# Attention steps placed between the quarters of the input projection's column blocks, and one ring for both kinds of weight halves

## The reference, cut to what matters

```python
def token_mixers(h, w_in_l, ...):                      # per layer
    gate_b, gate_c, u, q, k, v, g_conv, g_attn = jnp.split(h @ w_in_l, IN_SPLITS, axis=-1)
    y_conv = (gate_b * short_conv(gate_c * u, conv_w_l, conv_b_l)) @ w_conv_out_l
    ...                                                 # q, k rotated for the sample only
    o = rms_norm(diff_attention(q, k_all, v_all, lam), subln_g_l) * (1 - lam_init)
    y_attn = o.transpose(0, 2, 1, 3).reshape(b, n, ATTN_W) @ w_attn_out_l
    merged = jax.nn.sigmoid(g_conv) * y_conv + jax.nn.sigmoid(g_attn) * y_attn
    return merged @ w_out_l, k, v
```

## Time and profile before

| | |
|---|---|
| median of 3 runs | 1264.48 us (1263.8 to 1265.05) |
| the profiled execution | 1265.79 us, span 1264.0 us |
| PE busy | 1131.8 us, 90% of the span |
| DVE busy, ACT busy | 855.1 us (68%), 712.9 us (56%) |
| DMA | 332.56 MB, mean 263 GB/s |
| chain that ended last | PE 80%, DVE 7%, DMA 5%, ACT 4%, issue 3% |

### The profile page before, as it was taken

One profiled execution on the slowest core, in us unless ns is written; L12 is line 12 of the kernel. 1 busy time (PEld: TensorE's weight loads), 2 busy tenths in 40 slices (PEclk: granted clock), 3 DMA queues, 4 the chain that ended last, 5 costly groups with the idle time before them and its releaser, 6 DMA issues.

```text
span 1264.0 us, 15771 instructions
## 1 busy us (share of the span) xinstructions
PE 1131.8 (90%) x5573; PEld 910.0 (72%) x5573; DVE 855.1 (68%) x1227; ACT 712.9 (56%) x1018; POOL 149.4 (12%) x140
## 2 busy tenths in 40 slices
PE   4699999889799999799999989449999999999980
PEld 1588885468689889588886478438888788788870
DVE  1575686645675455585676845539889889889964
ACT  1444455534544444444445644538888888888862
POOL 5040002000360000340002000340000000000001
PEclk9799999999899999899999979769999999999995
DMA  9776657985259746565746964069999999999952
GB/s 327 285 262 231 200 168 270 386 325 185 92 164 410 274 160 204 148 203 197 233 166 216 387 212 152 0 227 337 375 381 384 373 381 383 373 388 378 375 211 100
DMA packets 165848, 332.56 MB, mean 263 GB/s; under 512 B 6528, under 2 KB 27120, under 8 KB 165792
## 3 DMA queue, kind: packets, MB, share of 16 engines
q1 hardware_dynamic: 158288, 307.78, 69.2%
q0 software_dynamic: 7472, 24.03, 5.6%
q10 hardware_dynamic: 32, 0.01, 0.0%
HBM read 314.48 MB, written 17.30 MB: 262 GB/s over the span
## 4 chain that ended last, share of the span: by engine, by line
PE 80%; DVE 7%; DMA 5%; ACT 4%; issue 3%; POOL 0%; SPq 0%; ACTq 0%; DVEq 0%; POOLq 0%
PE bank L1269 24%; PE bank L1271 23%; PE bank L1270 23%; DMA raw<-in_ada_w 4%; PE bank L1458 2%; ACT w_hi L534 2%; PE bank L1353 1%; DVE xT_lo L850 1%; PE bank L1413 1%; DVE x L863 1%; DVE w_lo L815 1%; ACT xT_hi L557 1%; PE bank L1561 1%; PE bank L1402 1%; PE bank L1582 1%
## 5 line engine op out<-in xcount | busy, mean ns | idle before, releaser
L815 DVE TENSOR_TENSOR w_lo<-raw,w_hi 128x1024 fp32r<-128x1024 f32 (+1 forms) x484 | 567.6, 1204 | 226.5 <-ACT w_hi L534 224.6
L534 ACT ACTIVATE w_hi<-raw 128x1024 fp32r<-128x1024 f32 (+1 forms) x504 | 500.2, 1008 | 359.4 <-PE bank L1271 359.1
L1269 PE MATMUL bank<-w_hi,xT_hi 128*128 128x512 f32 (+1 forms) x1056 | 409.4, 388 | 25.9 <-DVE w_lo L815 12.4
L1271 PE MATMUL bank<-w_lo,xT_hi 128*128 128x512 f32 (+1 forms) x1056 | 404.1, 383 | 0.0
L1270 PE MATMUL bank<-w_hi,xT_lo 128*128 128x512 f32 (+1 forms) x1056 | 403.9, 382 | 0.0
L1269 PEld LDWEIGHTS bank<-w_hi,xT_hi 128*128 128x128 f32 x1056 | 200.4, 190 | 67.4 <-issue 14.6
L1271 PEld LDWEIGHTS bank<-w_lo,xT_hi 128*128 128x128 f32 x1056 | 200.2, 190 | 35.1
L1270 PEld LDWEIGHTS bank<-w_hi,xT_lo 128*128 128x128 f32 x1056 | 200.7, 190 | 33.3
L1269 PE MATMUL bank<-w_hi,hT_hi 128*128 128x512 f32 x360 | 142.6, 396 | 3.4 <-issue 3.4
L1271 PE MATMUL bank<-w_lo,hT_hi 128*128 128x512 f32 x360 | 141.3, 392 | 0.0
L1270 PE MATMUL bank<-w_hi,hT_lo 128*128 128x512 f32 x360 | 141.0, 392 | 0.0
(11 more groups left out here) (233 smaller groups left out, 860.2 us busy)
## 6 DMA issues: line engine op xcount, KB each, us to landing
raw<-in_w_in SPq DMA_DIRECT2D x52, 1024.0 KB, 5.1
raw<-in_ada_w SPq DMA_DIRECT2D x48, 1024.0 KB, 11.4
raw<-in_moe_w_gate SPq DMA_DIRECT2D x32, 1024.0 KB, 7.4
raw<-in_moe_w_up SPq DMA_DIRECT2D x32, 1024.0 KB, 8.1
raw<-in_moe_w_down SPq DMA_DIRECT2D x32, 1024.0 KB, 7.9
raw<-in_moe_w_gate SPq DMA_DIRECT2D x16, 768.0 KB, 8.9
raw<-in_moe_w_up SPq DMA_DIRECT2D x16, 768.0 KB, 7.6
raw<-in_moe_w_down SPq DMA_DIRECT2D x16, 768.0 KB, 7.8
```

The lines of the kernel that those rows point to most:

```text
L534: nc.scalar.activation(w_hi[:, unit, 0:n], raw[:, r, at:at + n], ACT.Copy).then_inc(hi_done, 1)
L815: V.tensor_tensor(w_lo[:, unit, 0:n], raw[:, ring(q, s)[0], at:at + n], w_hi[:, unit, 0:n].bitcast(F32), ALU.subtract).then_inc(lo_done, 1)
L1269: pe.matmul(o, hi, wh, start=start, stop=False)
L1271: return pe.matmul(o, hi, wl, start=False, stop=stop)
```

## The change

The attention stage is gone. Each of the 13 blocks of `w_in` is taken in its four quarters, so that a layer has 52 quarters, numbered 0 to 51 (`tick` in the code; quarter `4*pos + unit`). From quarter 8 on every even quarter holds a step of the attention's pipeline, 20 steps in quarters 8 to 46; one step's work on PE is in two pieces, ahead of the quarter's matmuls (`step_begun`: score matmul 0 and p times V) and behind them (`step`: the transposes of q and k, score matmul 1, the transposes of p). The order of `w_in`'s blocks is now q, k, v, q, k, v, three convolution blocks, four gate blocks. The scores of both halves lie in one bank, p and the output in one bank, and so each job waits for the copies of the job before it. The ring is given out by halves in the order of use: in quarters 5 to 35 of layer 0 three of four hold a conditioning half, in layer 1 every odd one. The convolution's four chunks follow quarters 37, 39, 41 and 43. ACT's Sigmoid for the first gate block (`LATE_GATE`, block 9) comes behind the last exponential, in quarter 40. The amounts of arithmetic and of bytes stay.

```diff
+        qkT = sb("qkT", [P, 2, 3 * T])
...
-        def s_bank(j, i):
-
-            return bank[j % 2 + 6 * i]
+        QK, ADA, SCORES, PO = 2, 3, 4, 5
+
+        def scores(i):
+
+            return bank[SCORES][:, 2 * T * i:2 * T * (i + 1)]
...
+        STEP0, STEPS = 2 * PARTS, JOBS + 4
+        CONV0 = 9 * PARTS + 1
+        LATE_GATE = 9
+
+        def step_at(tick):
+            t = (tick - STEP0) // 2
+            return t if tick % 2 == 0 and 0 <= t < STEPS else None
...
+        def half_at(l, tick):
+            if not PARTS < tick < 9 * PARTS:
+                return None
+            if l == 0:
+                return None if tick % PARTS == 0 else 2 * QUAD * quads(l)[0] + tick // PARTS * 3 - 3 + tick % PARTS - 1
+            return None if tick % 2 == 0 else 2 * QUAD * quads(l)[0] + (tick - PARTS) // 2
...
+            needed = [(PARTS * (r - 1) + 2 * half, 0, ("weights", turn0[l] * SLOTS + r, half))
+                      for r in range(Q_LAYER * SLOTS) for half in range(2)]
+            for tick in range(PARTS * IN_BLOCKS):
+                n = half_at(l, tick)
+                if n is not None:
+                    needed.append((tick, 1, ("ada", n // 2, n % 2)))
+            stream += [entry for _, _, entry in sorted(needed)]
...
                 # ACT
+                for tick in range(PARTS * IN_BLOCKS):
+                    pos, unit = divmod(tick, PARTS)
+                    if unit == 0 and pos and pos - 1 != LATE_GATE:
+                        evacuated(pos - 1)
+                    hi(*slot(l, pos + 1), (unit,))
...
+                    if step_at(tick) is not None:
+                        step(step_at(tick))
+                    if tick == STEP0 + 2 * JOBS:
+                        evacuated(LATE_GATE)
+                    if quad_done(l, tick) is not None:
+                        ada_copy(quad_done(l, tick))
+                    if conv_at(tick - 1) is not None:
+                        conv_part(conv_at(tick - 1))
...
                 # DVE
+                    if step_at(tick) is not None:
+                        step_begun(step_at(tick))
+                    lo(*slot(l, pos + 1), (unit,))
+                    if step_at(tick) is not None:
+                        step(step_at(tick))
...
+                    if tick == CONV0 - 1:
...
+                        then(V.tensor_tensor(work[:, B_GC, :], work[:, B_GC, :], work[:, B_U, :], ALU.mult))
+                        dve.sem_inc(gcu_ok, 1)
+                    if conv_at(tick) is not None:
+                        conv(conv_at(tick))
+                    if conv_at(tick - 1) is not None:
+                        conv_rests(conv_at(tick - 1))
...
                 # PE
+                def step_begun(t):
+                    j = t - 1
+                    if 0 <= j < JOBS:
+                        pe.wait_ge(j_qkT, JOBS * l + j + 1)
+                        if j >= 1:
+                            pe.wait_ge(j_exp, JOBS * l + j)
+                        scored(j, 0).then_inc(j_s0, 1)
...
+                        if j >= 1:
+                            pe.wait_ge(j_oc, JOBS * l + j)
+                        for k in range(keys(j) // T):
+                            ins = pe.transpose(bank[PO][:, k * T:(k + 1) * T], p_buf[:, y, k * T:(k + 1) * T], ident[:, :])
+                        ins.then_inc(j_pT, 1)
...
+                    for unit in range(PARTS):
+                        tick = PARTS * pos + unit
+                        if step_at(tick) is not None:
+                            step_begun(step_at(tick))
+                        columns(*slot(l, pos), (unit,), outs, COL)
+                        if quad_turned(l, tick) is not None:
+                            i = quad_turned(l, tick)
+                            pe.wait_ge(j_pTc, JOBS * l + min((tick - STEP0) // 2 - 2, JOBS))
+                            ada_turn(i, bank[PO][:, 3 * T:3 * T + 4 * G * QUAD])
+                        if step_at(tick) is not None:
+                            step(step_at(tick))
+                        if half_at(l, tick) is not None:
+                            ada_half(half_at(l, tick))
+                        if conv_at(tick) is not None:
+                            conv_transposes(conv_at(tick))
```

More of the change, by code:

```diff
@@ new lines, in quad_done, with quad_turned, quads_kept @@
+        def quad_done(l, tick):
+            h = half_at(l, tick)
+            return None if h is None or h % (2 * QUAD) < 2 * QUAD - 1 else h // (2 * QUAD)
+        def quad_turned(l, tick):
+            if tick % 2 == 0:
+                return None
+            return quad_done(l, tick - 1) if quad_done(l, tick - 1) is not None else quad_done(l, tick - 2)
+        def quads_kept(l, tick):
+            return quads(l)[0] + sum(quad_turned(l, i) is not None for i in range(tick))
+        stream = [("ada", n // 2, n % 2) for n in range(2 * QUAD)]
@@ L278, in _, with free @@
         def _(sp):
[L279 to L282 removed]
+            def free(i):
+                if i >= 2 * SLOTS:
+                    kind, n, half = stream[i - 2 * SLOTS]
                     if kind == "ada":
[L284 removed]
+                        sp.wait_ge(ada_sum, 2 * n + half + 1)
                     else:
                         sp.wait_ge(lo_done, PARTS * n + 2 * half + 2)
[L288 to L294 removed]
@@ new lines, in source @@
+            def source(kind, n, half):
+                if kind == "ada":
+                    return columns(a["ada_w"][n // ADA_BLOCKS], half, n % ADA_BLOCKS * COL, COL)
+                l = int(n >= turn0[1] * SLOTS)
+                r = n - turn0[l] * SLOTS
+                if r < IN_BLOCKS:
+                    return columns(a["w_in"][l], half, ORDER_IN[r] * COL, COL)
+                if r < Q_LAYER * SLOTS:
+                    name, k0 = (("w_conv_out", 0), ("w_attn_out", 0), ("w_attn_out", 4), ("w_out", 0), ("w_out", 4))[r - IN_BLOCKS]
+                    return rows(a[name][l], half, k0, k0 + 4)
+                e, j = divmod(r - Q_LAYER * SLOTS, PER_EXPERT)
+                return expert_part(j, half, a["ffn_w_gate"][0][:, e * FF:(e + 1) * FF], a["ffn_w_up"][0][:, e * FF:(e + 1) * FF],
+                                   a["ffn_w_down"][0][e * FF:(e + 1) * FF, :])
@@ new lines, in _, with of, first_rows @@
+            for i, (kind, n, half) in enumerate(stream):
+                free(i)
+                r, part, _ = seat(i)
+                fill(r, part, *source(kind, n, half))
+            q = turn0[1] + Q_LAYER
+            def of(e):
+                return tuple(a[n][0, bass.ds(e, 1)].rearrange("e d f -> (e d) f")
+                        for n in ("moe_w_gate", "moe_w_up", "moe_w_down"))
+            def first_rows():
+                sp.wait_ge(x_sent, 16 * 2 * G)
+                x_load(0)
+                sp.wait_ge(gx_t, 1)
+                x_load(1)
```

590 lines of the change are left out of this document (253 added, 337 removed).

## The result

The changed kernel takes 1287.67 us (median of 4 runs, 1286.19 to 1291.82) beside 1264.14 us for the kernel before on the same chip: ratio 1.0185, 95% interval 1.0171 to 1.0199, 23.5 us slower. The prediction of 1272 us had the sign right and the size wrong; the time lies above its range (1255 to 1282). The profiled execution took 1288.15 us, span 1286.4 us, with PE busy for 1154.9 us (90%), DVE 856.0 (67%) and ACT 712.4 (55%).

A forecast was written before the change was run, and what follows sets the result against it. PE was taken as the bound, except in the attention stages, where it idles (layer 0's limited by DMA). Prize -27.5, (a) and (b) +15.6, waits +17.3, clock +1.9 gave +7.3 on 1264.5: 1272 us, range 1255 to 1282.

The forecast's parts named there:

- The prize: Both layers' attention stages: PE's idle time, a wait before the broadcast and slow matmuls afterwards go away, 27.5 us gained.
- (a): A job's two score matmuls no longer side by side on PE: 0.29 us more per job, 4.6 us per layer.
- (b): Each return of PE from float32 work to weight matmuls: 0.08 us, 40 returns, 3.2 us per layer.
- The waits: PE waiting on ACT and DVE, mostly in quarters 37 to 44 and at turns: 8.3 and 9.0, together 17.3 us.
- layer 1's two turns: PE's turns of `ada_turn` behind quarters 21 and 37 wait for DVE's copy of p's transposes, 1.0 us each.
- (c): PE's clock drops to the lower level after a wait of 4 us: 1.9 us, at even odds in each layer.
- The ring by halves: Weight ring and its DMAs, costed at nothing; PE waits 1 to 3 us if six halves don't bridge block 1.
- Rival 3: Each score matmul alone costs as much as the pair, in every even quarter: 10.6 us more, 1282.6 us; chance 0.13.
- Rival 1: Faster: ACT and DVE keep up in quarters 36 to 44, some 1.5 us waited per layer, 1255.6 us; chance 0.24.
- Rival 2: No change: waits of 5 us per layer and no clock loss, or lower (a), 1264.5 us; chance 0.15.
- Rival 4: Layer 0's weight ring runs dry on DMA in blocks 1 to 4, 6 us or more, 1278 us; chance 0.06.
- Exponentials and p come just in time: Up to quarter 35, while odd quarters hold a conditioning half, ACT's and DVE's answers reach PE without a wait.

The follow-up runs named there:

- The best version: `e13_dve_reordered` with the rotations of blocks 0 and 1 moved back to the odd quarter: 1250.1 us, ratio 0.9882 to the kernel before.
- e13_dve_reordered: Changed kernel with score pair ahead, later Sigmoids, early Sqrt table, and DVE's chunks, conditioning addition and rotations reordered: 1257.2 us, ratio 0.9933 to the kernel before.
- e3_one_score: The changed kernel without score matmul 1, both softmaxes reading matmul 0's scores: 1285.3 us, ratio 1.0160 to the kernel before.
- e9_step_first_one_score: The changed kernel with DVE's step ahead of `lo` and score matmul 1 left out: 1260.7 us, ratio 0.9977 to the kernel before.

## Why the prediction was wrong, step by step

**The prize, 27.5 us: right.** The best version has two layers 14.5 us shorter than before. It pays for its returns (about 0.16 x 80 = 12.8 us) and still waits some 2 us, so that the idle time won is about 29 us.

**(a), the two scores apart: the term that was mis-sized most, 9.2 us.** Each of the two takes alone what the pair takes (0.415 and 0.63 us), so that 0.52 us a job was due for the matmul alone where the sum had 0.29, gaps included. The balance below leaves 17 us for it. The experiments stand on both sides of that: a score left out gave 0.67 us a job, the pair kept together 0.43, 14 us. My reason for the low end, that the whole-array matmuls show no exposed weight load, does not bear on the question: each half of the pair was never cheap, the two ran at the same time. The prediction had cited a page of the Trainium skill for just this (TensorE: Matmul & The Clock Gate, "Why this matters for your kernels": slices of fewer than 128 rows run concurrently, one alone takes as long as a full-height one) and weighed it below a doubtful reading of rows; the trace agrees with the page as to the two running at once, 0.626 us for one and 0.63 for two.

**(b), 0.08 per return, 6.4 us in all: too low by half.** I read only the first interval behind a transpose. The whole return is 0.11 to 0.17, and 0.09 come ahead where a half or a score follows the weight matmuls: 0.16 to 0.17 a quarter, about 13 us.

**The waits, 17.3 us: right, mechanism and size.** Quarter 42 was put at 4.1 and took 3.9; 44 at 1.35 and took 1.35; 40 at 1.0 and took 0.6; layer 1's two turns at 1.0 and waited 0.7 each. PE's waits inside the two layers sum to 15.3 us.

**(c), 1.9 us at even odds: it came in both layers,** 2.2 us in each of the quarters 43 alone.

**Not in the sum:** the table load ahead of the norms (2.2 us). I had followed the load that the change adds ahead of the Sigmoids, not the one that is due when Sqrt comes back. The ring by halves was costed at nothing, and no run shows more: the stretch ahead of layer 0's `w_in`, 1.4 us shorter in the changed kernel, takes 43.8 to 45.3 us in the kernels with the new ring and 44.4, 45.5 and 46.7 in the three with the old.

With (a) as what is left over, the measured sum is -27.5 + 17 + 13 + 15.3 + 4.5 + 2.2 - 2.0 = +22.5 us, and 22.4 were measured between the spans. The prediction had +7.3: (a) and (b) are 14 us of the 15 that it missed, (c) and the table 5 more, the waits and the 2.0 won at the ends 4 less.

**The rivals.** Rival 3 (scores as dear as the pair), at 0.13, had the mechanism of (a), and its sign, single scores of 0.4 and 0.6 us, is what the trace shows; by the sum it alone gave 1282.6, and (b), (c) and the table lie beyond it. Rival 1 fell: ACT and DVE do not keep up in quarters 36 to 44. Rival 2 had neither the waits' full size nor the clock loss that came. Rival 4 did not come in the changed kernel, where no `w_in` quarter waits for `raw`; its kind of wait came once, in `e13_dve_reordered`, not by the DMA rate but because slots were freed late.

**What failed in the form of the sum.** The terms were added as if each stood alone. `e3_one_score` shows that they don't: with one score left out altogether the time was still 1285, so with (a) merely as cheap as I had it, it would have been no less, and not the 1280 that the sum gives. The turns and the exponentials would have been waited for, and the clock would have fallen behind the waits. "Exponentials and p come just in time" stood in the prediction; read on, it says that PE has no slack there to win. So the right price of (a) closes the balance, but (a) by itself did not put the time above the range: the price of the split and the way round through `lo` bind together, and only the edit of both (`e9_step_first_one_score`) gave the time back.

## What to carry to other kernels

Here a pair of matmuls on different rows of the array was one unit of time (0.63 us for two, 0.63 for one): before splitting such a pair over two places, price each half as the whole pair. When a dependent chain is spread between the parts of a dense stream, draw the way round through every queue that it crosses and put each answer ahead of the instruction that waits for the stream (`hi`, `lo`), not behind it; only then does PE's saving show. The idea of the change was sound (1.2% faster in the end): its order and the split pair were what cost 3% against that.

## What the runs showed of the hardware that I had not expected

DVE and POOL hinder each other: a rotation's `tensor_tensor` with two operands in SBUF took 2.6 us beside POOL's and 0.41 without it. The Trainium skill (GPSIMD Engine Reference, "Specifications") says that POOL's SBUF interfaces are shared with VectorE, with contention for instructions with two SBUF inputs; here the trace agrees, and the price is a wait for nearly the whole of POOL's instruction.

Leaving the weight matmuls for float32 work and coming back has a price on both sides. The return costs 0.11 to 0.17 us, much the same behind one transpose, p times V, a score or a conditioning half; another 0.09 comes ahead when the work that follows has 32 columns or 64 rows (0.32 us behind the last weight matmul and not 0.23).

The granted clock cannot be read off the length of one wait: behind a wait of 1.5 us it fell to the lower level (`e3_one_score`, quarters 37 and 38 of both layers), and behind one of 2.8 us it did not (`e9_step_first_one_score`, quarters 42 and 43 of both layers).
